# One full-width subtract on GpSimd in place of four quarter-width ones

## The chip, the cores and the metric

The kernel runs on one core of one Trainium2 chip. The metric is the time of one execution on the device in microseconds (us), the median of several runs; lower is better.

## The reference, cut to what matters

The reference computes four transformer-like layers on a sequence of 512 tokens with model width 1024, all in float32: a state-space (S5) layer with a gated output, a sliding-window attention layer with sinks, a layer with retention and a short convolution, and a latent-attention layer. Each of the first two also has an MLP (`relu` squared, width 4096) and a gated extra input. What matters here is that nearly all the arithmetic is products of activations with large float32 weight matrices:

```python
mix = s5_mixer(hn, ...)                                   # ends in y @ w_glu
h = h + jnp.square(jax.nn.relu(hm @ w_up[i])) @ w_down[i]
gate = jax.nn.sigmoid(rmsnorm(h, norm_ple[i]) @ w_ple_gate[i])
h = h + gate * (p[i] @ w_ple_proj[i])
...
q, k, v, g_ret, cb, cc, cx, g_conv = split_cols(h @ w_in, EVEN_SPLITS)
```

## The kernel before, in words

**Products in three passes.** TensorE is given float32 values split in two parts. A weight strip of 128 partitions x 1024 columns arrives in `raw`; ScalarE copies it to the rounded type `whi` (L455), and GpSimd subtracts, `wlo = raw - whi` (L424). Activations are split the same way (`Ah`/`Al`, `Bh`/`Bl`, `Ch`/`Cl`, `Lh`/`Ll`: the high part by ScalarE at L476 or L478, the low part by VectorE at L1343 or L1345). Each product is then three matmuls, high x high (L799), high x low (L800), low x high (L801). A strip is 24 matmuls of 128x512.

**The ring.** There are 288 strips and four slots (`RING = 4`). Each engine has its program written out by hand in its own block, with semaphores between them. For strip t the SyncE queue loads `raw` once `lo_ready` tells that the slot's last subtract has ended; ScalarE splits it (`split_strip`) once TensorE has finished the strip that used the slot's `whi`; GpSimd's `low_strip` waits for `hi_ready`, subtracts in four parts of 256 columns and raises `lo_ready` with the last one; TensorE's `strip` waits for `lo_ready` and for a free PSUM bank (`evac`). ScalarE splits a strip three strips ahead of its use (`LEAD = 3`).

**Stages that the prediction speaks of.** In order of time:
- the S5 stage: VectorE prepares matrices (L319 to L321) and scans (L1264 to L1278); the first strip is split during it. GpSimd also splits a small tensor `P` in two parts of 128x512 (L431);
- `glu`: its first strip needs all eight tiles of `Al` (L1396), which VectorE makes at its start;
- `gate0` and `gate1`: for each of eight tiles m, VectorE scales the product (L1366), ScalarE takes its sigmoid and then splits the next strip, VectorE multiplies (`ev<-sg,ple`, L1480) and adds to `h` (L1481), ScalarE makes the high part and a square, and VectorE makes the low parts (L1345) and adds the square (L1355; in `gate1` a second sum at L1467). The first strip of the stage behind needs the low part of tile 7;
- the window attention: 32 units, two or three steps ahead of each other. For each, VectorE adds the mask (L1509), takes a maximum (L1511), and later divides in two instructions (L1522, L1523); TensorE then transposes (L998) and multiplies by the values (L977). Between units TensorE does quarters of the `q` strips (`strip_part`);
- `even`: 56 strips; in the last 32 VectorE's convolution (L1650 to L1652, L1659) and retention (L1633 to L1635) go between them, and `eout` begins with the convolution's last tile;
- `odd` and `qb`: VectorE makes `Ll` tiles (L1345), sums of squares (L1355), a reciprocal root (L1361), and with it scales the outputs of `qb` (L1366).

The four parts of one subtract, and where they stand in GpSimd's program:

Of the kernel before, what the change touches and what calls it, by code (L numbers as in the profile page):

```python
# [7 lines left out]
F32 = mybir.dt.float32  # L8
FR = mybir.dt.float32r
I32 = mybir.dt.int32  # L10
ALU = mybir.AluOpType
# [5 lines left out]
D = 1024  # L17
# [105 lines left out]
def program(nc, a):  # L123

    with ExitStack() as top:
        def sem(name):
            return top.enter_context(nc.semaphore(name))

        def area(stack, name, shape, dt=F32):
            return stack.enter_context(nc.sbuf_tensor(name, shape, dt))  # L130
# [4 lines left out]
        raw = area(top, "raw", [P, RING, D])  # L135
# [38 lines left out]
        whi = area(main, "whi", [P, RING, D], FR)  # L174
        wlo = area(main, "wlo", [P, RING, D], FR)
# [66 lines left out]
        lo_ready = sem("lo_ready")  # L242
# [173 lines left out]
        @block.gpsimd  # L416
        def _(pool):
            nc.gpsimd.memset(T[:, :, :, :], 0.0).then_inc(t_zero, 1)

            def low_strip(i, r):  # L420
                pool.wait_ge(hi_ready, RING * i + r + 1)
                for part in range(4):
                    cc = slice(part * D // 4, (part + 1) * D // 4)
                    last = nc.gpsimd.tensor_tensor(wlo[:, r, cc], raw[:, r, cc], whi[:, r, cc].bitcast(F32), ALU.subtract)  # L424
                last.then_inc(lo_ready, 1)


            low_strip(0, 0)
            for k in range(2):
                pool.wait_ge(x_hi, XT["p0"] + k + 1)  # L430
                nc.gpsimd.tensor_tensor(X["P"][1][:, k, :], p_raw[:, k, :], X["P"][0][:, k, :].bitcast(F32), ALU.subtract).then_inc(x_lo, 1)  # L431

            for r in range(1, RING):
                low_strip(0, r)
            with pool.Fori(1, NS // RING) as i:
                for r in range(RING):
                    low_strip(i, r)
# [1458 lines left out]
```

## Time and profile before

| | |
|---|---|
| time, median of 3 runs | 2059.63 us (2059.45 to 2060.03) |
| time of the profiled execution | 2060.03 us |
| its span, first to last instruction | 2057.5 us |
| TensorE matmul busy | 1959.6 us (95%) |
| VectorE / ScalarE / GpSimd busy | 934.9 / 747.6 / 880.1 us |
| mean granted TensorE clock | 0.952 |
| weight strips | 288, with 1152 subtracts on GpSimd |

In the profile PE is TensorE's matmuls, PEld its weight loads, DVE is VectorE, ACT is ScalarE and POOL is GpSimd. L424 is line 424 of the kernel. "Releaser" is what ended an engine's idle time. The profile is of one execution; its times are used for the sums.

### The profile page before, as it was taken

The page shows a single profiled execution, that of the slowest core. Times are in us where ns is not written, and L with a number is a line of the kernel's source. Part 1 is how long each engine was busy: PE and PEld are TensorE (multiplying, and loading weights), DVE is VectorE, ACT ScalarE, POOL GpSimd, SP SyncE. Part 2 cuts the span into 40 slices and gives each one's busy share as a digit, 9 for nine tenths or more (in the row PEclk, how much of TensorE's full clock was granted, in tenths as well). Part 3 has the DMA queues.
Part 4 walks back from the last instruction along what each step waited for, and adds up shares of the span by engine and source line. Part 5 has one row for each costly group of instructions (what it writes and reads, how often), then busy time and mean ns, then how long its engine had stood idle before and what let it go on. Part 6 is the DMA issues. An engine that isn't in the chain of part 4 may idle for free.

```text
span 2057.5 us, 25021 instructions
## 1 busy us (share of the span) xinstructions
PE 1959.6 (95%) x8728; PEld 1577.0 (77%) x8728; DVE 934.9 (45%) x1444; ACT 747.6 (36%) x1172; POOL 880.1 (43%) x1159
## 2 busy tenths in 40 slices
PE   2999999999999899999999999899999999899996
PEld 1888888888888666688888888787887878586674
DVE  7995232121226578642221215742255551556554
ACT  7223333232324445534332324422233342333561
POOL 1042555555555511245555555554444445262221
PEclk8556999999999999999999999999999999899998
DMA  3245333333333300123323332232222223131111
GB/s 136 52 129 151 105 95 99 102 92 92 102 92 92 111 30 31 32 85 109 97 97 95 95 97 84 82 101 82 86 78 82 74 79 96 60 111 46 42 41 41
DMA packets 59296, 175.24 MB, mean 85 GB/s; under 512 B 14784, under 2 KB 15168, under 8 KB 58560
## 3 DMA queue, kind: packets, MB, share of 16 engines
q1 hardware_dynamic: 57344, 170.34, 27.5%
q10 hardware_dynamic: 1872, 3.80, 0.6%
q8 instruction: 54, 0.88, 0.2%
q14 instruction: 26, 0.21, 0.0%
HBM read 163.37 MB, written 4.19 MB: 81 GB/s over the span
## 4 chain that ended last, share of the span: by engine, by line
PE 85%; DVE 9%; ACT 3%; issue 1%; DMA 1%; SPq 0%; DVEq 0%; ACTq 0%
PE ps L799 24%; PE ps L801 23%; PE ps L800 23%; PE ps L860 1%; PE ps L862 1%; PE ps L958 1%; PE ps L977 1%; PE ps L1131 1%; PE ps L929 1%; PE ps L925 1%; PE ps L1130 1%; PE ps L1140 1%; PE ps L914 1%; DVE rstd L1361 1%; DVE h L1481 1%
## 5 line engine op out<-in xcount | busy, mean ns | idle before, releaser
L424 POOL TENSOR_TENSOR wlo<-raw,whi 128x256 fp32r<-128x256 f32 x1152 | 869.8, 787 | 1135.1 <-ACT whi L455 1135.1
L455 ACT ACTIVATE whi<-raw 128x1024 fp32r<-128x1024 f32 x288 | 302.1, 1052 | 394.1 <-PE ps L801 386.8
L799 PE MATMUL ps<-Ch,whi 128*128 128x512 f32 x912 | 364.8, 400 | 5.5 <-DVE Cl L1345 5.4
L801 PE MATMUL ps<-Ch,wlo 128*128 128x512 f32 x912 | 356.5, 391 | 0.0
L800 PE MATMUL ps<-Cl,whi 128*128 128x512 f32 x912 | 356.3, 391 | 0.0
L799 PE MATMUL ps<-Ah,whi 128*128 128x512 f32 x656 | 265.8, 405 | 15.0 <-DVE Al L1345 11.5
L801 PE MATMUL ps<-Ah,wlo 128*128 128x512 f32 x656 | 257.1, 392 | 0.0
L800 PE MATMUL ps<-Al,whi 128*128 128x512 f32 x656 | 256.8, 391 | 0.0
L799 PE MATMUL ps<-Bh,whi 128*128 128x512 f32 x640 | 250.9, 392 | 0.0
L801 PE MATMUL ps<-Bh,wlo 128*128 128x512 f32 x640 | 249.3, 390 | 0.0
L800 PE MATMUL ps<-Bl,whi 128*128 128x512 f32 x640 | 249.2, 389 | 0.0
L799 PEld LDWEIGHTS ps<-Ch,whi 128*128 128x128 f32 x912 | 171.8, 188 | 49.2 <-issue 6.7
L801 PEld LDWEIGHTS ps<-Ch,wlo 128*128 128x128 f32 x912 | 171.8, 188 | 36.4
L800 PEld LDWEIGHTS ps<-Cl,whi 128*128 128x128 f32 x912 | 172.1, 189 | 35.4 <-issue 1.4
L799 PEld LDWEIGHTS ps<-Ah,whi 128*128 128x128 f32 x656 | 124.3, 189 | 48.1 <-issue 11.8
L800 PEld LDWEIGHTS ps<-Al,whi 128*128 128x128 f32 x656 | 124.1, 189 | 26.7 <-issue 2.8
L801 PEld LDWEIGHTS ps<-Ah,wlo 128*128 128x128 f32 x656 | 123.9, 189 | 26.2
L799 PEld LDWEIGHTS ps<-Bh,whi 128*128 128x128 f32 x640 | 120.2, 188 | 25.8 <-issue 1.0
L800 PEld LDWEIGHTS ps<-Bl,whi 128*128 128x128 f32 x640 | 120.2, 188 | 25.7 <-issue 1.0
L801 PEld LDWEIGHTS ps<-Bh,wlo 128*128 128x128 f32 x640 | 120.2, 188 | 25.0
L1435 DVE TENSOR_TENSOR h<-ps,h 128x512 f32 x48 | 33.2, 692 | 216.4 <-PE ps L801 216.4
L1426 DVE SCALAR_TENSOR_TENSOR ev<-ps,rstd 128x512 f32<-128x512 f32 x64 | 44.3, 692 | 166.8 <-PE ps L801 166.3
(330 smaller groups left out, 2300.5 us busy)
## 6 DMA issues: line engine op xcount, KB each, us to landing
raw<-in_w SPq DMA_DIRECT2D x288, 512.0 KB, 3.6
u<-in_xch SPq DMA_DIRECT2D x1, 2048.0 KB, 11.8
yg<-vsb SPq DMA_DIRECT2D x16, 128.0 KB, 2.3
yg<-z SPq DMA_DIRECT2D x16, 128.0 KB, 2.3
ysc<-yg ACTq DMA_DIRECT2D x8, 256.0 KB, 2.0
h<-in_xfm SPq DMA_DIRECT2D x2, 1024.0 KB, 6.2
out<-h SPq DMA_DIRECT2D x8, 256.0 KB, 2.0
bB<-in_bc SPq DMA_DIRECT2D x1, 1024.0 KB, 7.3
```

The costliest lines, as they stand in the source:

```text
L424: last = nc.gpsimd.tensor_tensor(wlo[:, r, cc], raw[:, r, cc], whi[:, r, cc].bitcast(F32), ALU.subtract)
L455: nc.scalar.activation(whi[:, slot, :], raw[:, slot, :], ACT.Copy).then_inc(hi_ready, 1)
L799: nc.tensor.matmul(out, whi[:, slot, w], xh, start=first, stop=False)
L800: nc.tensor.matmul(out, whi[:, slot, w], xl, start=False, stop=False)
L801: return nc.tensor.matmul(out, wlo[:, slot, w], xh, start=False, stop=last)
L860: nc.tensor.matmul(ps[:, 2 + sl % 2, g * NC:(g + 1) * NC], T[:, gg // (GR // 2), :, gg % (GR // 2)], u[:, gg, :], start=True, stop=False)
L862: last = nc.tensor.matmul(ps[:, 2 + sl % 2, g * NC:(g + 1) * NC], out_place(sl)[:, g, :], S[:, gg, :], start=False, stop=True)
L914: nc.tensor.matmul(ps[:, bank, :], C("ones"), acc[:, :] if src is None else src, start=True, stop=True).then_inc(nrm_ps, 1)
L925: nc.tensor.matmul(ps[:, bank, :], C(perm), src, start=True, stop=True).then_inc(rope_ps, 1)
L929: last = nc.tensor.transpose(ps[:, bank, k * P:(k + 1) * P], src[:, k * P:(k + 1) * P], C("ident"))
L1426: V.scalar_tensor_tensor(ev[:, 0, :], bank(name, j), 0.0, rstd[:, :], ALU.max, ALU.mult).then_inc(evac, 1)
L1435: V.tensor_tensor(h[:, o, :], bank(name, j), h[:, o, :], ALU.add).then_inc(evac, 1)
```

## The change

The four subtracts of 128x256 in `low_strip` become one of 128x1024. The semaphore is raised by that one. Nothing else changes: the same elements are computed, on the same engine, behind the same wait.

```diff
             def low_strip(i, r):
                 pool.wait_ge(hi_ready, RING * i + r + 1)
-                for part in range(4):
-                    cc = slice(part * D // 4, (part + 1) * D // 4)
-                    last = nc.gpsimd.tensor_tensor(wlo[:, r, cc], raw[:, r, cc], whi[:, r, cc].bitcast(F32), ALU.subtract)
-                last.then_inc(lo_ready, 1)
+                nc.gpsimd.tensor_tensor(wlo[:, r, :], raw[:, r, :], whi[:, r, :].bitcast(F32), ALU.subtract).then_inc(lo_ready, 1)
```

## Rows read from the trace of the kernel before

**Rows 1.** The page: span, busy times and instructions, chain by engine.

```profile
span 2057.5 us, 25021 instructions
PE 1959.6 (95%) x8728; PEld 1577.0 (77%) x8728; DVE 934.9 (45%) x1444; ACT 747.6 (36%) x1172; POOL 880.1 (43%) x1159
...
PE 85%; DVE 9%; ACT 3%; issue 1%; DMA 1%; SPq 0%; DVEq 0%; ACTq 0%
```

**Rows 2.** L424 by source line (ns min/median/max) and who waited; one uncontested burst.

```profile
L424 POOL TENSOR_TENSOR wlo<-raw,whi x1152: 722/743/1821, 114.9 to 2019.2; 128x256 fp32r<-128x256 f32 x192
...
  PEld ps L799: 0.5, 2
...
1486.91 2.85 POOL L424 TENSOR_TENSOR wlo<-raw,whi 128x256 fp32r<-128x256 f32 x4 [5.24 <-ACT whi L455]
```

**Rows 3.** Source lines (ns min/median/max) of VectorE and of GpSimd's wider subtract.

```profile
L431 POOL TENSOR_TENSOR Pl<-tab,Ph x2: 1540/1626/1711, 123.3 to 124.8; 128x512 fp32r<-128x512 f32 x2
...
L1275 DVE TENSOR_TENSOR z<-Wc,z x8: 683/684/1759, 67.1 to 135.1; 128x512 f32<-128x512 f32 x8
...
L320 DVE TENSOR_TENSOR bt<-pwi,bC x8: 1214/1486/1761, 121.2 to 164.6; 128x1024 f32<-128x1024 f32 x8
...
L1522 DVE TENSOR_SCALAR sm<-sm,cols x32: 352/354/852, 730.0 to 855.0; 128x256 f32<-128x256 f32 x32
```

**Rows 4.** Timelines of GpSimd and VectorE in the S5 stage (start us, us).

```profile
114.92 4.18 POOL L424 TENSOR_TENSOR wlo<-raw,whi 128x256 fp32r<-128x256 f32 x4 [107.25 <-ACT whi L455]
...
117.39 1.11 DVE L1267 TENSOR_TENSOR z<-z 128x512 f32<-128x512 f32 x1
```

**Rows 5.** Timelines at the first strip of glu.

```profile
198.91 3.28 POOL L424 TENSOR_TENSOR wlo<-raw,whi 128x256 fp32r<-128x256 f32 x3 [37.86 <-ACT whi L455]
...
199.89 1.04 DVE L1396 TENSOR_TENSOR Al<-yfm,Ah 128x512 fp32r<-128x512 f32 x1
...
200.99 0.50 PE L799 MATMUL ps<-Ah,whi 128*128 128x512 f32 x1 [0.58 <-DVE Al L1396]
```

**Rows 6.** Timelines at the ends of gate0 and of gate1.

```profile
678.15 1.12 DVE L1481 TENSOR_TENSOR h<-h,ev 128x512 f32<-128x512 f32 x1
...
680.07 1.06 DVE L1345 SCALAR_TENSOR_TENSOR Al<-h,gp,Ah 128x512 fp32r<-128x512 f32 x1
681.05 1.23 DVE L1345 SCALAR_TENSOR_TENSOR Cl<-h,gp,Ch 128x512 fp32r<-128x512 f32 x1
...
683.52 0.69 DVE L1481 TENSOR_TENSOR h<-h,ev 128x512 f32<-128x512 f32 x1
...
685.87 0.79 PE L799 MATMUL ps<-Ah,whi 128*128 128x512 f32 x1 [3.72 <-DVE Al L1345]
...
1316.63 0.80 PE L799 MATMUL ps<-Ch,whi 128*128 128x512 f32 x1 [3.83 <-DVE Cl L1345]
```

**Rows 7.** Timelines of one unit of the window attention.

```profile
743.16 2.92 POOL L424 TENSOR_TENSOR wlo<-raw,whi 128x256 fp32r<-128x256 f32 x4 [25.90 <-ACT whi L455]
...
743.98 0.82 DVE L1523 TENSOR_SCALAR sm<-sm,cols 128x256 f32<-128x256 f32 x1
...
745.09 0.66 PE L998 MATMUL ps<-cst,sm 128*128 128x128 f32 x4
```

**Rows 8.** Timelines before eout.

```profile
1670.84 3.77 POOL L424 TENSOR_TENSOR wlo<-raw,whi 128x256 fp32r<-128x256 f32 x4 [3.82 <-ACT whi L455]
...
1671.49 1.12 DVE L1652 TENSOR_TENSOR cy<-cy,ev 128x512 f32<-128x512 f32 x1
...
1681.01 0.50 PE L799 MATMUL ps<-Ah,whi 128*128 128x512 f32 x1 [1.61 <-DVE Al L1343]
```

**Rows 9.** Timeline of VectorE before qb.

```profile
1822.19 1.23 DVE L1345 SCALAR_TENSOR_TENSOR Ll<-kn,gp,Lh 128x512 fp32r<-128x512 f32 x1
```

**Rows 10.** Windows: PE, PEld, DVE, ACT, POOL busy, then PEclk.

```profile
723.00:856.00 133.00, 127.07 (x624) 86.88 (x624) 110.20 (x291) 67.67 (x204) 17.47 (x24) 0.97 0.08 25
...
686.00:691.00 5.00, 5.00 (x10) 3.14 (x11) 2.10 (x3) 3.12 (x5) 0.03 (x1) 0.50 0.56 184
```

## Prediction

> **What bounds the kernel now.** I read the page first: TensorE is busy for 1959.6 of 2057.5 us and holds 85% of the chain that ended last, VectorE 9% of it [rows 1]. So the end moves only where TensorE waits, or where it runs at its lower clock. Next, the changed line itself: 1152 subtracts of 743 ns in the median, and of all TensorE's waits only 0.5 us is put down to them [rows 2]. A strip passes GpSimd in 2.85 us when nothing disturbs it [rows 2], while TensorE needs 24 matmuls for it, over 5 us. GpSimd's own speed is therefore worth nothing here, and a faster subtract brings no gain by itself. What is left is what the subtracts do to others. For that I read the durations of single lines on VectorE as minimum, median and maximum: instructions of one shape come in two sorts, a short one and one that is longer by a fixed amount [rows 3], and the timelines show that the long ones are those that lie beside a subtract [rows 4 to 9]. The 9% of the chain on VectorE is where this counts.
>
> **The cost of one collision.** A VectorE instruction that reads two tensors of SBUF (or one, in the forms of L1522 and L1523) and meets a subtract of 256 columns is longer by 0.50 us on L1522 (852 against 352 ns) [rows 3], by 0.42 on L1267 (1.11 against 0.69 for its shape) [rows 4] and by 0.43 on L1652 (1.12 against 0.69) [rows 8]; GpSimd's subtract in turn lasts up to 1.8 us instead of 0.74 [rows 2]. They take turns: one VectorE instruction, one subtract. What a wider subtract costs the trace shows once: L431 has 512 columns, and the VectorE line beside it, L1275, goes from 684 to 1759 ns, 1.07 us longer; L320, whose record overlaps its predecessor in the same way, is longer by 0.54 beside a subtract of 256 (1761 against 1218) [rows 3]. So 256 more columns add 0.53 us to the wait. For 1024 columns that makes 0.43 + 3 x 0.53 = 2.02 us for one wait, and 0.74 + 3 x 0.53 = 2.33 us for the subtract. The low bound is four waits of 0.43, 1.72 us; the high one L1522's 0.50 + 1.59 = 2.09.
>
> The row for L1275 shows that VectorE stood still for the longer part of a 512-column subtract. The Trainium skill, "SBUF — State Buffer", section "Who interferes with whom", has the rule behind it: the port pair that GpSimd shares with VectorE is an exclusive lock, held for the whole instruction, and a VectorE instruction with two SBUF inputs contends with a GpSimd one that reads SBUF. The rule speaks against this change: it turns four short locks with gaps between them into a long one. By that rule taken literally a wait would be the whole 2.33 us, and the sum below about 2 us larger; by the row it is 2.02.
>
> So GpSimd is free 0.5 us earlier for each strip (2.85 to 2.33), which nobody waits for. VectorE waits once for 2.02 us where it waited up to four times for 0.43. Where VectorE works densely it had four such waits, 1.7 us, and little changes; where one or two of its instructions met a subtract, each strip costs it up to 1.6 us more. What that costs TensorE, place by place:
>
> - **S5 stage.** Four VectorE instructions wait beside the first strip's four subtracts [rows 4], some 1.7 us together; one wait of 2.02 takes their place, and TensorE waits for the matrices behind: +0.3.
> - **glu.** GpSimd starts at 198.91 and VectorE's seventh tile ends at 199.38, so the long subtract holds VectorE from there until 201.4. The eighth tile (1.04 us from 199.89) ends at 202.4 instead of 200.93, and TensorE stands waiting for it already, 0.58 us [rows 5]: +1.5.
> - **gate0.** The chain is VectorE's from tile to tile; TensorE has 3.72 us idle at the end for the last low part [rows 6]. From the end of one `h` (679.27) to the next (684.21) is 4.94 us, in which `Al` is 0.31 and `Cl` 0.48 over their undisturbed 0.75, so 4.15 without waits. The eight tiles took 37.85 us from the first `h` (645.67 + 0.69) to the last, thus 8.8 us of waits over seven strips. With one long subtract each, I follow the order of the engines: the sigmoid and the split (1.05 us) put GpSimd's start about 1.8 us behind L1366, so it falls by turns behind `h`, where VectorE would have idled 0.8 us for ScalarE anyway (a wait of 1.25), and between two dense instructions (2.02). Four of 1.25 and three of 2.02 make 11.1: +2.3.
> - **Window attention.** 24 subtracts, six strips, fall in it [rows 10], and the six collisions look alike. GpSimd starts at 743.16; L1522 waits 0.50 and L1523 0.47 (0.82 against 0.35), ending at 744.80; TensorE transposes at 745.09 [rows 7], which leaves 0.24 us of slack when 0.05 for the semaphore is taken off. With the long subtract L1522 waits 2.09 and L1523 not at all: 1.12 later, less the slack is 0.88. TensorE is the pace there (127 of 133 us busy [rows 10]) and doesn't make it up: 6 x 0.88 = +5.3.
> - **gate1.** As gate0, with 3.83 us idle at its end [rows 6] and an instruction more per tile; 8.3 us of waits become 11.1: +2.8. Behind it one product of two SBUF tensors (L1569) may meet a second long subtract, within 0.1 us: 0 or +1.7, and I take 0.
> - **even to eout.** L1652 waits for the first subtract of the strip that starts at 1670.84; it will wait 2.02 for 0.43, and a chain through two divisions and the convolution leads from it to TensorE, which waits 1.61 us for it already [rows 8]: +1.6. In the seven earlier passes TensorE has other strips to do.
> - **qb.** `Ll` waits once more, and the sum of squares ahead of it; the last `Ll` (end 1823.42 [rows 9]) comes 1.3 later, the scale with it, and TensorE needs the first bank 0.1 us after it is free: +1.2.
> - **Clock.** After gate0's wait of 3.72 us [rows 6] the granted clock was 0.50, the lower of the two levels of 1.2 and 2.4 GHz, at least from 686 to 691 [rows 10]. TensorE's wait before eout grows from 1.61 to 3.2 us, nearer to that one: I take one stretch of 3.4 us at the lower level, +1.7, bounded by 0 and twice that.
>
> Elsewhere (up and down strips, kvb, the latent attention) the instructions that meet a subtract have over 1 us before TensorE needs them, and I cost them at nothing; without that cover each strip would cost 1.6. The sum is 0.3 + 1.5 + 2.3 + 5.3 + 2.8 + 1.6 + 1.2 + 1.7 = 16.7 us on the profiled 2060.03, which stands 0.4 above the median; from the median it gives 2059.6 + 16.7 = 2076.3, so 2076. With the low bound of the wait every place loses 0.3 and the attention 6 x 0.3, together about 4, so 2072 and without the clock's term 2070.
>
> **The rivals.** *Faster, by shorter waits.* If VectorE had to wait only for some part of a long subtract, about as long as for 256 columns now, it would meet fewer of them, as GpSimd works 2.33 us a strip instead of 2.85: about one wait of 0.43 less for each tile of the gates, 6 us, less 0.4 at the start, 2053. It decides if a wait stays below 0.5 us. Against it stands the 1.07 us beside 512 columns [rows 3]. 0.05.
>
> *No change.* The collisions move to where VectorE has slack: a start that comes 0.1 us later falls into a reciprocal of 3.3 us that doesn't contend. It needs the phases of GpSimd and VectorE to shift in most places, though both follow the same strip ends. Gates at their old waits and the attention hidden leaves 0 to 4 us: 2060 to 2063. 0.09. A half way, with the attention's stalls taken up, is 2064 to 2068, 0.06.
>
> *More, by the clock.* Six stalls of 0.88 us in the attention, each with 3.4 us at the lower clock behind it, cost 1.7 each, 10 us more: 2086. For it speaks that TensorE's many short idles there have already given 0.97 of the clock over the stage [rows 10]; against it, that a stall of 0.9 is far shorter than the 3.72 of gate0. With L1569's 1.7 the case reaches 2092. 0.2.
>
> **How the numbers follow.** The forecast, 2069 to 2083, has 0.6. A change of 0.2% (4 us) is about what a measurement of this kernel can tell from none. Slower: 0.6 + 0.2 + 0.06 = 0.86; the same 0.09; faster 0.05. The range goes from 2065, which leaves out the two cases at the low end and part of the third, to 2091 in the clock case: some 0.18 outside.
>
> **What would show it.** In the changed kernel's trace: 288 subtracts of at least 2.3 us each; VectorE's long sort at 1.7 to 2.1 us over the short one, and fewer of them; L1522 at 2.4 us six times, with TensorE waiting 0.9 us at L998 behind each; idle ahead of the first matmuls of kv, `even` and eout about 6, 6 and 3.2 us in all. The step most likely wrong is the attention's, as its slack is only 0.24 us and its order is decided by 0.05; after it the turns within the gates. Waits of 0.4 us beside long subtracts would make the whole prediction wrong.

## Result: 2090.64 us, slower by 1.5%

The changed kernel takes 2090.64 us in the median (2090.03 to 2092.38, 4 runs), the one before 2059.83 beside it on the same chip (2059.45 to 2060.37, 4 runs): a ratio of 1.0151, with a 95% interval of 1.0136 to 1.0166. Run again later, on another occasion, it gave 2090.3 and 1.0151. The forecast was 2076.0, with a range of 2065 to 2091: the sign is right and the time is within the range, near its upper end, but the growth is 30.8 us where 16.4 were forecast.

The page of the changed kernel, its head and the line of the subtract (L422, L424 in before). Behind the change its line numbers are three lower than those of before:

```profile
span 2087.8 us, 24157 instructions
PE 1966.3 (94%) x8728; PEld 1578.9 (76%) x8728; DVE 979.6 (47%) x1444; ACT 746.9 (36%) x1172; POOL 723.8 (35%) x295
...
PE 81%; DVE 12%; ACT 3%; issue 2%; DMA 1%; SPq 1%; DVEq 0%; ACTq 0%
...
L422 POOL TENSOR_TENSOR wlo<-raw,whi 128x1024 fp32r<-128x1024 f32 x288 | 712.9, 2478 | 1319.8 <-ACT whi L452 1319.8
```

GpSimd is 156 us less busy than in [rows 1] and nobody gains by it. VectorE's part of the chain is 12% where it was 9%, VectorE is busy for 44.7 us more with the same 1444 instructions (the profile counts the time that an instruction waits beside a subtract as busy), and TensorE has 6.7 us more too: the same matmuls, more of them at the lower clock.

By source line (minimum, median and maximum in ns): the subtract, the first division in the attention (L1522 in [rows 3], L1519 here), and two others of VectorE:

```profile
L422 POOL TENSOR_TENSOR wlo<-raw,whi x288: 2387/2426/3505, 115.0 to 2047.4; 128x1024 fp32r<-128x1024 f32 x144
...
L1519 DVE TENSOR_SCALAR sm<-sm,cols x32: 352/354/2529, 737.4 to 867.4; 128x256 f32<-128x256 f32 x32
...
L1478 DVE TENSOR_TENSOR h<-h,ev x16: 691/694/2805, 650.3 to 1334.1; 128x512 f32<-128x512 f32 x16
...
L1648 DVE SCALAR_TENSOR_TENSOR cy<-cu,gp,cy x8: 752/2801/2806, 1502.1 to 1694.6; 128x512 f32<-128x512 f32 x8
```

One subtract is 2.43 us (2.33 forecast), and a VectorE instruction that meets it is longer by 2.05 (L1648, 2.806 less 0.752), 2.11 (`h`, 2.805 less 0.694) or 2.18 us (L1519, 2.529 less 0.354), where 2.02 was forecast and 2.09 the bound. So the price of one collision held, within some 0.1 us. To see where the 30 us arise I matched VectorE's instructions of the two traces, one by one in their order, and read how much later each starts in the changed kernel. The steps of that shift lie at a few places:

| place | shift grows by | forecast |
|---|---|---|
| S5 stage | 3.1, of which 0.8 by the clock | 0.3 |
| glu | 1.5 | 1.5 |
| gate0, with the clock behind it | 2.8 | 2.3 |
| window attention | 5.9, of which 0.9 is given back by the clock | 5.3 |
| gate1 | 7.5 | 2.8 |
| first strip behind gate1, with the clock | 4.1 | 0 (bound 1.7) |
| even to eout | 1.7, then 2.8 and 0.7 by the clock | 1.6 |
| qb | 1.3 | 1.2 |
| clock | (in the places above) | 1.7 |

These steps and small ones between them, both ways, make the 30.3 us by which the span grows.

**S5.** VectorE's timeline, a line of GpSimd's and one of TensorE's:

```profile
142.69 3.32 DVE L321 TENSOR_TENSOR E<-E,bt 128x1024 f32<-128x1024 f32 x1
...
146.05 3.31 DVE L319 TENSOR_TENSOR E<-pwr,bC 128x1024 f32<-128x1024 f32 x1
...
149.28 3.43 DVE L320 TENSOR_TENSOR bt<-pwi,bC 128x1024 f32<-128x1024 f32 x1
...
141.43 10.20 POOL L422 TENSOR_TENSOR wlo<-raw,whi 128x1024 fp32r<-128x1024 f32 x3 [14.32 <-ACT whi L452]
...
146.07 0.69 PE L857 MATMUL ps<-u,T 128*128 128x64 f32 x2 [1.41 <-DVE E L321]
```

The forecast looked only at the first strip's subtract. The next three strips of the ring are subtracted in one burst of 10.2 us from 141.43, in the middle of the output matrices, and three VectorE instructions wait there. Of before, the same instruction and what it took:

```profile
142.03 1.65 DVE L321 TENSOR_TENSOR E<-E,bt 128x1024 f32<-128x1024 f32 x1
```

TensorE needed that matrix at once in before too, but had it just in time; now it stands for 1.41 us, and for 0.86 at a matrix behind. The rest of the 3.1 us is a stretch at the lower clock that lasts 51.2 us there where it lasted 47.8.

**glu and gate0** went as worked out, gate0 in part by luck. TensorE at glu's first strip (0.58 us in [rows 5]), and VectorE and GpSimd at two tiles of gate0:

```profile
205.59 0.50 PE L796 MATMUL ps<-Ah,whi 128*128 128x512 f32 x1 [2.08 <-DVE Al L1393]
...
662.07 0.69 DVE L1478 TENSOR_TENSOR h<-h,ev 128x512 f32<-128x512 f32 x1
663.56 2.04 DVE L1342 SCALAR_TENSOR_TENSOR Al<-h,gp,Ah 128x512 fp32r<-128x512 f32 x1
...
666.78 2.91 DVE L1477 TENSOR_TENSOR ev<-sg,ple 128x512 f32<-128x512 f32 x1
...
662.07 2.98 POOL L422 TENSOR_TENSOR wlo<-raw,whi 128x1024 fp32r<-128x1024 f32 x1 [4.72 <-ACT whi L452]
...
666.21 2.94 POOL L422 TENSOR_TENSOR wlo<-raw,whi 128x1024 fp32r<-128x1024 f32 x1 [1.16 <-ACT whi L452]
```

The subtract falls by turns behind `h`, where `Al` loses 1.29 (2.04 against 0.75), and among dense instructions, where `ev` loses over 2.1. TensorE's waits from 640 to 700, which were one of 3.7 in before:

```profile
PE ps L796 <- DVE Al L1342: 6.0, 2, 3.5
```

These turns hang on a tie: at 662.07 the subtract and `h` start together, and `h` runs through. Three such ties in this trace all go to VectorE. In the trace of the same kernel taken later one of three goes to GpSimd, and TensorE's first wait at the end of gate0 is then 4.5 instead of 3.5 us:

```profile
684.77 2.88 DVE L1481 TENSOR_TENSOR h<-h,ev 128x512 f32<-128x512 f32 x1
...
684.76 2.34 POOL L424 TENSOR_TENSOR wlo<-raw,whi 128x1024 fp32r<-128x1024 f32 x1 [4.71 <-ACT whi L455]
```

So gate0's term differs by about 1 us from one execution to the next, and the forecast didn't have the tie.

**gate1** is the largest miss. The same two engines there, then TensorE's waits (us in total, times, longest) from 1300 to 1365:

```profile
1299.59 0.69 DVE L1477 TENSOR_TENSOR ev<-sg,ple 128x512 f32<-128x512 f32 x1
1300.31 2.81 DVE L1478 TENSOR_TENSOR h<-h,ev 128x512 f32<-128x512 f32 x1
...
1307.10 2.80 DVE L1478 TENSOR_TENSOR h<-h,ev 128x512 f32<-128x512 f32 x1
```

```profile
1299.77 2.79 POOL L422 TENSOR_TENSOR wlo<-raw,whi 128x1024 fp32r<-128x1024 f32 x1 [4.72 <-ACT whi L452]
...
1306.56 2.79 POOL L422 TENSOR_TENSOR wlo<-raw,whi 128x1024 fp32r<-128x1024 f32 x1 [4.00 <-ACT whi L452]
```

```profile
PE ps L796 <- DVE Cl L1342: 11.9, 3, 5.7
PE ps L796 <- DVE q L1363: 2.1, 1, 2.1
```

From the third tile on there are no turns: GpSimd starts about 0.54 us before the addition to `h` (1299.77 against 1300.31, 1306.56 against 1307.10), while `ev` still runs; the subtract lasts 0.4 us over its 2.4, and the addition waits for its end. Five tiles in a row pay the whole 2.1 us on the chain. TensorE waits 11.9 us for `Cl` where the same view of before has 5.4 us in two waits. The last line is its wait for `q`, which hangs on the product of two SBUF tensors behind the stage (L1569 before, L1566 now): that product met a second subtract and took 2.95 us instead of 0.99. The forecast named this and costed it at nothing.

**Window attention.** TensorE's waits for the second division (us in total, times, longest), in before and in the changed kernel:

```profile
PE ps L998 <- DVE sm L1523: 5.9, 6, 1.5
```

```profile
PE ps L995 <- DVE sm L1520: 11.8, 14, 1.6
```

Six new stalls of 0.86 to 0.88 us make 5.3 of the 5.9 us more. The rest is 0.57 us at 859, where before ran at the lower clock from 841.8 to 845.2 and had no wait: the clock gives back 0.9 there, and this wait takes part of it again. One of the six, where [rows 7] had none:

```profile
750.55 2.42 POOL L422 TENSOR_TENSOR wlo<-raw,whi 128x1024 fp32r<-128x1024 f32 x1 [27.25 <-ACT whi L452]
...
750.59 2.53 DVE L1519 TENSOR_SCALAR sm<-sm,cols 128x256 f32<-128x256 f32 x1
...
753.44 0.66 PE L995 MATMUL ps<-cst,sm 128*128 128x128 f32 x4 [0.88 <-DVE sm L1520]
```

**eout and the clock.** TensorE's wait before eout (1.61 in [rows 8]), and two windows behind it (busy us of PE, PEld, DVE, ACT, POOL, then the granted clock):

```profile
1706.61 0.80 PE L796 MATMUL ps<-Ah,whi 128*128 128x512 f32 x1 [3.28 <-DVE Al L1340]
```

```profile
1707.00:1712.00 5.00, 5.00 (x13) 3.84 (x13) 4.86 (x9) 4.82 (x8) 1.05 (x1) 0.50 0.01 3
1713.00:1718.00 5.00, 5.00 (x24) 4.10 (x23) 1.39 (x2) 1.42 (x2) 3.04 (x2) 1.00 0.48 128
```

TensorE is busy for all of both windows, with 13 matmuls in one and 24 in the other: that is what the lower level (0.50, 1.2 GHz) costs. The lower level held for 6.8 us here, where before had no such stretch. At the gates the stretches of 6.8 and 3.4 us became 10.2 and 13.7, and a new one of 3.4 lies behind the wait of 2.1.

### The profile page after: what moved, and what is told of

The parts are those of the page before. It is cut to its first block, busy times and chain, and to the rows that moved or that the text cites. A ratio compares the mean times of both kernels' runs of the same rounds, so it can differ in the third digit from the quotient of the medians.

```text
span 2087.8 us, 24157 instructions
## 1 busy us (share of the span) xinstructions
PE 1966.3 (94%) x8728; PEld 1578.9 (76%) x8728; DVE 979.6 (47%) x1444; ACT 746.9 (36%) x1172; POOL 723.8 (35%) x295
## 4 chain that ended last, share of the span: by engine, by line
PE 81%; DVE 12%; ACT 3%; issue 2%; DMA 1%; SPq 1%; DVEq 0%; ACTq 0%
PE ps L796 23%; PE ps L798 23%; PE ps L797 23%; PE ps L1128 1%; PE ps L926 1%; DVE h L1478 1%; DVE ev L1477 1%; PE ps L922 1%; PE ps L955 1%; PE ps L1127 1%; PE ps L911 1%; PE ps L857 1%; PE ps L1137 1%; PE ps L859 1%; DVE rstd L1358 1%
## 5 line engine op out<-in xcount | busy, mean ns | idle before, releaser
L422 POOL TENSOR_TENSOR wlo<-raw,whi 128x1024 fp32r<-128x1024 f32 x288 | 712.9, 2478 | 1319.8 <-ACT whi L452 1319.8
L796 PE MATMUL ps<-Ch,whi 128*128 128x512 f32 x912 | 366.6, 402 | 14.0 <-DVE Cl L1342 11.9
```

Source lines behind the costliest of these rows:

```text
L422: nc.gpsimd.tensor_tensor(wlo[:, r, :], raw[:, r, :], whi[:, r, :].bitcast(F32), ALU.subtract).then_inc(lo_ready, 1)
L796: nc.tensor.matmul(out, whi[:, slot, w], xh, start=first, stop=False)
```

## The experiments

The theory, A: everything comes from VectorE's waits, each as long as the rest of the GpSimd instruction that it meets, at places where TensorE is waiting for VectorE. Rivals: the wait isn't set by the width, GpSimd's being at work or its start counts, or the loss is mostly one stage's.

**Two halves and eight eighths.** The width by itself:

```diff
-                for part in range(4):
-                    cc = slice(part * D // 4, (part + 1) * D // 4)
+                for part in range(2):
+                    cc = slice(part * D // 2, (part + 1) * D // 2)
```

> Two subtracts of 128x512 for each strip. Theory A (VectorE and GpSimd take turns, and a wait lasts as long as the subtract that is met: 0.43 us for 256 columns and 0.53 for each 256 more): VectorE's waits are 0.96 to 1.07 us, two of them where it works densely; in the window attention L1519 and L1520 (the two divisions) wait for one each, so they end as late as beside one full-width subtract; the whole comes to 2077 (2070 to 2084). Theory B (the cost goes in proportion to the width beyond 256 columns): a third of the change's 30.8 us, 2070. Theory C (only full-width subtracts outlast VectorE's gaps, narrower ones are absorbed): 2060 to 2062.

> Eight subtracts of 128x128 for each strip. Theory A (turns; a wait lasts as long as the subtract that is met): waits of about 0.2 us, and the kernel is faster than with four, 2055 (2050 to 2059); GpSimd needs 3.6 to 4 us a strip, still under the 5.4 of TensorE. Rival (each collision has a fixed price of 0.43 us, and their number counts): twice as many waits in the gates and the S5 stage, 2070 or more. Rival (eight instructions make GpSimd the bound): TensorE waits for wlo, far over 2060.

Halves: 2073.59 us (2069.13 to 2075.89) against 2059.38, a ratio of 1.0075 (1.0058 to 1.0092). Eighths: 2055.67 (2054.66 to 2060.83), 0.9985 (0.9974 to 0.9996). The division in the attention and the convolution's last addition, with halves and then with eighths:

```profile
L1522 DVE TENSOR_SCALAR sm<-sm,cols x32: 352/353/1418, 731.4 to 860.8; 128x256 f32<-128x256 f32 x32
...
L1652 DVE TENSOR_TENSOR cy<-cy,ev x8: 1685/1686/1686, 1487.1 to 1678.8; 128x512 f32<-128x512 f32 x8
```

```profile
L1522 DVE TENSOR_SCALAR sm<-sm,cols x32: 352/354/572, 728.8 to 852.8; 128x256 f32<-128x256 f32 x32
...
L1652 DVE TENSOR_TENSOR cy<-cy,ev x8: 835/839/839, 1475.7 to 1668.2; 128x512 f32<-128x512 f32 x8
```

With 0.691 undisturbed, the addition waits 0.15 us beside 128 columns, 0.43 beside 256 [rows 8] and 0.99 beside 512; beside 1024 `h`, of the same shape, waits 2.11: about 0.28 us for each 128 columns more. Time goes the same way, though for eighths only just clear of the noise. The width sets the wait, in the attention, the gates and the convolution alike; a theory in which only the number of collisions counts has eighths slower. The time of the halves alone decides less: it lies between the 2077 of theory A and the 2070 of theory B.

**Quarters in one stage only.** Three kernels keep the full width everywhere but at one place, where the strips are subtracted in four parts again. For the attention and gate1 the loop is written out; S5's strips 1 to 3 stand ahead of the loop, and `low_strip(0, r, 4)` does for them.

```diff
+            apart = {S0['q'] + m + LEAD for m in range(2, 8)}
...
+                        low_strip(g, r, 4 if RING * g + r in apart else 1)
```

> The changed kernel, with four parts again for the six strips that are split during the window attention only. Theory A (each place's loss is its own and TensorE never makes it up): 5.0 to 5.9 us less than the changed kernel, 2085 to 2086, and the six waits of 0.88 us at the transposes are gone. Rival (the attention's stalls are made up behind it, or the loss lies in the clock): within 1 us of the changed kernel's 2090.6.

> The changed kernel, with four parts again for the eleven strips that are split during gate1 and just behind it. Theory A: gate1's 7.5 us and the 4.1 us behind it (the product L1566 and the clock) come back, 2079 (2077 to 2081). Rival (gate1's large loss comes from a phase that earlier strips set, not from its own subtracts): less than half of it, 2085 or more.

> The changed kernel, with four parts again for strips 1 to 3, which are split while VectorE makes the S5 stage's output matrices. Theory A (VectorE was just in time there, and three long waits made TensorE wait 1.4 and 0.9 us): 2.3 to 2.8 us less than the changed kernel, 2088. Rival (the loss there comes from strip 0 or is hidden behind the later wait in glu): under 0.5 us less.

The attention in quarters: 2084.46 us (2081.6 to 2090.5), 1.012 (1.0103 to 1.0136), 5.8 to 6.2 us below the full width's 2090.3 to 2090.6. The profiled execution is its slowest, of 2090.5, but its waits at the transposes are back at before's 5.9 in 6 or less:

```profile
  DVE sm L1535: 4.6, 5
```

What makes this execution slow lies elsewhere: three ties in gate0 go to GpSimd, and TensorE is at the lower clock for 6.8 us behind glu's wait and for 13.7 us from 853.2, where the full width's trace has no such stretch.

gate1 in quarters: 2080.41 (2077.69 to 2085.56), 1.0113 (1.0096 to 1.013), 10.2 us below. TensorE's last wait there is 3.85 us, that of [rows 6], and the one behind the stage is gone:

```profile
1329.13 0.80 PE L811 MATMUL ps<-Ch,whi 128*128 128x512 f32 x1 [3.85 <-DVE Cl L1357]
```

S5's strips 1 to 3 in quarters: 2088.5 (2086.55 to 2090.44), 1.0125 (1.0105 to 1.0145), 2 us below. VectorE and TensorE there:

```profile
142.76 1.65 DVE L321 TENSOR_TENSOR E<-E,bt 128x1024 f32<-128x1024 f32 x1
...
144.47 0.65 PE L860 MATMUL ps<-u,T 128*128 128x64 f32 x2 [0.40 <-DVE E L321]
```

Of TensorE's two stalls there the first is 0.40 us instead of 1.41 and the second is gone; a stretch of 3.4 us at the lower clock behind glu's wait, which the full width's trace hasn't, takes part of the gain back. The three kernels give back 18 of the 31 us, each about what its stage had lost. gate1's 10.2 lies between its own 7.5 and the 11.6 with what follows it. Ranges of these runs overlap in part, so 2 us for S5 rests as much on its rows as on the times.

**GpSimd that doesn't read.** Is it the reads that collide, or GpSimd's being at work? Here the low part of the weights is left out but for 16 columns; the rest is filled with zeros by four fills that write as much and read nothing:

```diff
-                nc.gpsimd.tensor_tensor(wlo[:, r, :], raw[:, r, :], whi[:, r, :].bitcast(F32), ALU.subtract).then_inc(lo_ready, 1)
+                nc.gpsimd.tensor_tensor(wlo[:, r, 0:16], raw[:, r, 0:16], whi[:, r, 0:16].bitcast(F32), ALU.subtract)
+                for part in range(4):
+                    last = nc.gpsimd.memset(wlo[:, r, 16 + part * 252:16 + (part + 1) * 252].bitcast(F32), 0.0)
+                last.then_inc(lo_ready, 1)
```

> GpSimd computes only the first 16 columns of each low part and fills the other 1008 with zeros in four memsets of 252 columns: it is busy and writes as before, but hardly reads SBUF. The low part of the weights is left out of the result. Theory A (VectorE waits for GpSimd's reads): the long sort of VectorE instructions is gone, the contention of the kernel before too, so 2048 (2042 to 2053) and no wait over 0.1 us. Rival (VectorE waits for whatever GpSimd does with SBUF, writes too): waits of 0.2 to 0.3 us stay, 2054 to 2060.

2043.42 us (2042.52 to 2043.82), 0.9904 (0.9885 to 0.9923): nearly all collisions together cost before some 16 us, with the clock: the four stretches at the lower level that before has in and behind the gates and in the attention, 17 us long in all, are gone. Three lines of VectorE:

```profile
L1481 DVE TENSOR_TENSOR h<-h,ev x16: 691/692/693, 642.9 to 1299.2; 128x512 f32<-128x512 f32 x16
...
L1652 DVE TENSOR_TENSOR cy<-cy,ev x8: 691/691/691, 1462.2 to 1654.8; 128x512 f32<-128x512 f32 x8
...
L1522 DVE TENSOR_SCALAR sm<-sm,cols x32: 352/354/1325, 722.0 to 844.6; 128x256 f32<-128x256 f32 x32
```

Instructions with two tensors in SBUF never waited beside the fills. L1522, with one, did, by up to 0.97 us, which is longer than any one fill (0.45 at most): at 751.09 it stands through all four of them. These are two kinds of collision: the first with GpSimd's reads, the second with its writes too. The Trainium skill, "SBUF — State Buffer", section "Who interferes with whom", says just that: two SBUF inputs contend with a GpSimd instruction that reads SBUF and not with one that only writes, while the two-port modes that `tensor_scalar` can enter contend with any. By that rule, the trace agrees (0.693 us at most for the one, 1.325 for the other).

**The gates' temporaries in PSUM.** If the operand decides, then moving one operand out of SBUF must do what narrow subtracts do, at any width. In both gates the sigmoid, the product and the squares go to three free PSUM banks:

```diff
-                    answer(nc.scalar.activation(sg[:, :], ev[:, 0, :], ACT.Sigmoid))
+                    answer(nc.scalar.activation(ps[:, SX, :], ev[:, 0, :], ACT.Sigmoid))
...
-                        ch.link(V.tensor_tensor(ev[:, 1, :], sg[:, :], ple[:, m, :], ALU.mult))
-                        ask(V.tensor_tensor(h[:, m, :], h[:, m, :], ev[:, 1, :], ALU.add))
+                        ch.link(V.tensor_tensor(ps[:, SX, :], ps[:, SX, :], ple[:, m, :], ALU.mult))
+                        ask(V.tensor_tensor(h[:, m, :], h[:, m, :], ps[:, SX, :], ALU.add))
...
-                V.tensor_tensor(acc[:, :], acc[:, :], sq[:, :], ALU.add)
+                V.tensor_tensor(acc[:, :], acc[:, :], ps[:, SZ, :], ALU.add)
```

> The kernel before (four parts), with the gates' three temporaries (sigmoid and its product, both squares) in idle PSUM banks, so that three or four VectorE instructions of each tile read one SBUF tensor only. Theory A (only instructions with two SBUF inputs wait): those never wait, only the low parts do, and the gates get shorter: 2053 (2049 to 2057). Rival (the waits move to the low parts and stay as many): within 2 us of 2059.8.

> The changed kernel with the same temporaries in PSUM. Theory A: the long waits of the gates fall on the low parts alone, or on nothing: the gates give back 8 us or more of their 10.3, 2081 (2076 to 2084), and gate0 and gate1 have no wait of 2.1 us at the addition to h. Rival (a wait of 2.1 us simply moves to the low part of each tile): 2088 to 2091.

With quarters: 2051.72 us (2046.22 to 2053.54), 0.9947 (0.9926 to 0.9967). With the full width: 2065.83 (2062.11 to 2073.09), 1.0026 (1.0011 to 1.0042). TensorE's waits in the full-width kernel from 678 to 700 (with one of 0.3 for a sum) and from 1300 to 1350, and `h` in it:

```profile
PE ps L799 <- DVE Al L1345: 1.0, 1, 1.0
...
PE ps L799 <- DVE q L1366: 2.1, 1, 2.1
PE ps L799 <- DVE Cl L1345: 1.0, 1, 1.0
```

```profile
L1481 DVE TENSOR_TENSOR h<-h,ps x16: 686/689/690, 651.0 to 1313.1; 128x512 f32<-128x512 f32 x16
```

`h` no longer waits beside 1024 columns, although GpSimd starts 0.5 us ahead of it in gate1 as in the changed kernel, so the mechanism holds. The size was missed: the same edit gives back 24.8 us at the full width, where 8 to 14 were expected. The waits in the gates are 4.4 us instead of the full width's 20.0 (6.0, 11.9 and 2.1), which is 15.6; they are also below before's own 9.3, which the expectation hadn't counted. Of the rest, 9 us, the trace shows that the lower-clock stretches of 10.2, 13.7 and 3.4 us are gone, and so is that of 3.4 in the attention, while that of 6.8 at eout is 3.4; how the 9 us divide over them wasn't taken apart. The 2.1 us of the product behind gate1, which has both operands in SBUF, stayed.

**Both together, and narrower still.**

> Both improvements together: eight subtracts of 128x128 for each strip and the gates' temporaries in PSUM. Theory A: the gates are already at TensorE's pace with the temporaries in PSUM alone, so the eighths add only what they gain outside the gates (the attention's slack gains nothing; eout 0.3, glu nothing): 2051 (2048 to 2053), beside 2051.7 with four parts and 2043.4 with next to no reads.

> Sixteen subtracts of 128x64 for each strip, and the gates' temporaries in PSUM. A subtract of 128 columns takes 0.46 us alone and 279 ns less than one of 256, so one of 64 some 0.32, and a strip 4.5 to 5 us, just under TensorE's 5.4. Theory A: waits of at most 0.1 us, 2045 (2043 to 2048), as with eighths. Rival (GpSimd becomes the bound in the S5 stage and where two strips come together): TensorE waits for wlo, 2050 or more.

Eighths with the temporaries in PSUM: 2046.21 us (2044.91 to 2054.52) against 2059.97, 0.9949 (0.9932 to 0.9965). It has the lowest median of all kernels that compute the whole result, 13.8 us below before, 2.8 above the one whose GpSimd hardly reads, and below the 2048 to 2053 that was expected. Its ratio's interval overlaps that of the quarters (0.9926 to 0.9967), so a gain of the eighths on top of the temporaries isn't shown. Sixteenths, with the same temporaries: 2065.88 (2063.96 to 2068.16), 1.0035 (1.0022 to 1.0047), 20 us worse. The page of the sixteenths, its line of the subtract, a stretch of GpSimd's timeline and one of VectorE's:

```profile
PE 1960.1 (95%) x8728; PEld 1574.7 (76%) x8728; DVE 964.0 (47%) x1444; ACT 747.4 (36%) x1172; POOL 1413.6 (69%) x4615
...
L424 POOL TENSOR_TENSOR wlo<-raw,whi x4608: 308/324/1406, 115.8 to 2024.4; 128x64 fp32r<-128x64 f32 x192
```

```profile
659.82 3.39 POOL L424 TENSOR_TENSOR wlo<-raw,whi 128x64 fp32r<-128x64 f32 x10
```

```profile
659.68 3.35 DVE L1345 SCALAR_TENSOR_TENSOR Al<-h,gp,Ah 128x512 fp32r<-128x512 f32 x1
```

Sixteen subtracts of 0.324 us are 5.2 us, about what TensorE needs for a strip, so in the gates GpSimd is hardly ever out of work. And the low part, 0.75 us undisturbed, takes 3.35: nine subtracts ran through meanwhile and a tenth had begun, so VectorE was passed over again and again. "One VectorE instruction, one subtract", as the forecast had it, is not a rule. TensorE's waits at the ends of the gates are 3.3 and 5.3 us, where eighths have 1.0 and 1.0. No wait of TensorE's for `wlo` is seen, so the time is the rival's but its mechanism isn't what happened. Whether the passing over comes of the width or of GpSimd's having no gap isn't told apart.

**The split in gate1 later.** If GpSimd's start 0.54 us ahead of the addition costs gate1 its turns, a later start might bring them back. ScalarE gets one more copy ahead of each split there, at the full width:

```diff
+                    if layer == 1:
+                        nc.scalar.activation(X["A"][0][:, m, :], rcos[:, :], ACT.Copy)
                     if m + 1 < KT:
                         ahead(f"gate{layer}", m + 1)
```

> The changed kernel, but in gate1 ScalarE makes a copy of 128x512 (about 0.6 us, its result is used by nobody) between the sigmoid and the split of the next strip, so that GpSimd starts 0.6 us later. Theory (in gate1 GpSimd took the port 0.5 us before the addition to h asked for it, in each tile from the third on, so the whole 2.1 us fell on the addition; started behind it, 0.8 of it falls into VectorE's own idle time): faster than the changed kernel by 0.8 for each of some five tiles and what the clock gives back, 2085 (2081 to 2088). Rival (the turns don't matter, more work on ScalarE only makes the chain longer): 2090 to 2096.

> The changed kernel once more, on the chip of the two beside it, as their measure: 2090 (2088 to 2093).

The full width again gave 2090.3 (2088.88 to 2091.11), 1.0151 (1.0134 to 1.0168); with the later split 2091.67 (2088.94 to 2094.97), 1.0153 (1.0136 to 1.017). Nothing was gained. The two engines in gate1:

```profile
1305.03 2.94 DVE L1483 TENSOR_TENSOR h<-h,ev 128x512 f32<-128x512 f32 x1
```

```profile
1305.01 2.42 POOL L424 TENSOR_TENSOR wlo<-raw,whi 128x1024 fp32r<-128x1024 f32 x1 [5.24 <-ACT whi L455]
```

From one addition to the next it is 6.93 us, where the full width has 6.78. The delay was too short by a hair: GpSimd now comes 0.02 us ahead, and `h` waits 2.25 of the subtract's 2.42. The time is that of the rival, but the experiment doesn't decide whether the start's phase can save gate1; no longer delay was tried.

## Why the prediction was half right

**Right.** The sign; that GpSimd's own speed is worth nothing (156 us less, no gain); the price of a collision (2.05 to 2.18 against 2.02, up to 0.09 above the bound of 2.09, and below the subtract's whole 2.43); glu, +1.5 for +1.5; the attention, where six stalls of 0.88 us were forecast and came, 5.3 us of 5.9 in all, confirmed by quarters there giving back about 6; gate0's alternation and its +2.8 for +2.3, 0.6 of it the clock's, though its ties could have gone the other way; eout's wait, +1.7 for +1.6; qb, +1.3 for +1.2. These terms, 11.9 us of the sum, measured 13.2. One side sum was off: by the prediction's own low bound 0.3 us of wait is worth about 4 us of time, so a wait of the whole 2.33 would have added about 4, not 2.

**Wrong: "S5 stage ... +0.3".** The step counted the first strip and stopped. Strips 1 to 3 are subtracted in one burst beside the output matrices, where TensorE takes each matrix as soon as it is there. It measured 3.1, 2.3 of it TensorE's two stalls, and quarters for those three strips alone leave 0.4 of them.

**Wrong: "gate1. As gate0 ... +2.8".** The alternation of gate0 was carried over to a chain with one instruction more per tile. There the phase locks at 0.54 us ahead of the addition, and every tile pays 2.1: 7.5 us. The forecast's own premise, that phases decide, called for following gate1's order by itself.

**Wrong: "0 or +1.7, and I take 0", behind gate1.** The product met the subtract, 2.0 us, and the lower clock behind gate1's wait and behind this one made 2.1 more; together 4.1.

**Mis-sized: the clock, +1.7.** It came at more places than one. By TensorE's busy time for the same matmuls it is 0.8 us in S5, 0.6 at gate0, 1.0 in gate1 and 2.1 behind it, and 3.0 at eout and past it, less 0.9 in the attention. Together that is nearly all of the 6.7 us by which TensorE is busy longer. The rival in which the attention's stalls each bring a stretch did not come about: the attention had one stretch of 3.4 us, fewer than before's two. The range reached up to 2091 for that rival's sake, and the time lies in it by another way, 0.4 us below its end: that is luck.

## What to carry to other kernels

Where VectorE is on the path and GpSimd works beside it, the length of one GpSimd instruction is a latency for VectorE, so a fused instruction that saves GpSimd's time can cost the kernel. Narrow parts helped here down to 128 columns; at 64, where GpSimd had hardly a gap left, the kernel was slower again. Moving one of the two SBUF operands of `h` to PSUM took its wait away at each of the four widths tried, 64 to 1024 columns. And a forecast of collisions has to follow each dense stretch of VectorE by itself, the bursts of the start included: two stages of one form had different phases and different prices.

## What the runs showed of the hardware that was not expected

- A VectorE instruction can be passed over many times: 3.35 us for 0.75 of work, while GpSimd did nine subtracts of 128x64 and began a tenth.
- When the two ask together, the turn is unsteady. In gate0 both start at 662.07 and VectorE ran at its undisturbed 0.69; in the same kernel's later trace GpSimd, 0.01 us ahead at 684.76, won and `h` took 2.88.
- `tensor_scalar` with a single tensor input waits beside fills that only write (1.325 against 0.354 us), while `tensor_tensor` with two does not (0.691).
- A wait of 2.1 us, shorter than the 3.7 of [rows 6], can be followed by the lower clock, and needn't be. The wait of 2.1 behind gate1 brought 3.4 us of it. The wait at glu, 2.05 to 2.09 us in each of these, brought none in the changed kernel, 3.4 us with S5's strips in quarters and 6.8 with the attention's. These stretches are part of what puts that last execution at 2090.5 us where its kernel's median is 2084.46.
